# A two-layer hybrid decoder trunk: weight splits and evacuations reordered on the vector engine, expert rows turned one chunk later, a GpSimd multiplication in another form

## What is computed

```python
for l in range(DEPTH):
    h = rmsnorm(x, norm_mix[l])
    qa, ka, va, qb, kb, vb, qi, ki, wi, qc, kc, vc, g = _split(h @ w_in[l], IN_SIZES)
    o_a = stick_breaking_attention(...)       # 4 heads
    o_b = dsa_attention(...)                  # indexer picks the top 64 keys of each query
    o_c = sliding_window_attention(...)       # 8 heads, window 128, learned sinks
    merged = gate0 * (o_a @ w_pa[l]) + gate1 * (o_b @ w_pb[l]) + gate2 * (o_c @ w_pc[l])
    x = x + merged @ w_out[l]
    x = x + cross_attention(...)              # 4 heads into 256 memory tokens
    hf = rmsnorm(x, norm_ffn[l])
    x = x + (swiglu(hf, ...) if l % 2 == 0 else moe_swiglu(hf, ...))   # top 2 of 8 experts
```

## Time and profile before

| | |
|---|---|
| median of 3 runs | 1763.64 us (1762.31 to 1764.25) |
| the profiled execution | 1761.99 us, span 1760.4 us |
| PE busy | 1702.5 us, 97% |
| DVE busy | 1391.7 us, 79% |
| ACT busy | 1104.0 us, 63% |
| POOL busy | 92.9 us, 5% |
| mean transfer rate | 283 GB/s, 366 to 399 GB/s in most slices of the expert loop |

### The profile page before, as it was taken

One profiled execution on the slowest core, in us unless ns is written; L12 is line 12 of the kernel. 1 busy time (PEld: TensorE's weight loads), 2 busy tenths in 40 slices (PEclk: granted clock), 3 DMA queues, 4 the chain that ended last, 5 costly groups with the idle time before them and its releaser, 6 DMA issues.

```text
span 1760.4 us, 22594 instructions
## 1 busy us (share of the span) xinstructions
PE 1702.5 (97%) x7816; PEld 1366.5 (78%) x7816; DVE 1391.7 (79%) x1367; ACT 1104.0 (63%) x1076; POOL 92.9 (5%) x73
## 2 busy tenths in 40 slices
PE   7999898999999999899999999999999999999999
PEld 5777777888777787777888888888888888888876
DVE  5799767545477987668898888888888888888897
ACT  4646355443355453557777777777777777777765
POOL 1100110000001001010000000000000000000440
PEclk9999999999999999999999999999999999999999
DMA  8533494554455335349999999999999999999985
GB/s 301 215 104 130 176 364 149 212 191 169 150 182 182 120 138 204 134 173 399 366 381 366 366 381 369 366 383 365 364 385 363 381 363 368 380 367 366 409 340 195
DMA packets 74113, 498.14 MB, mean 283 GB/s; under 512 B 8256, under 2 KB 9024, under 8 KB 17872
## 3 DMA queue, kind: packets, MB, share of 16 engines
q1 hardware_dynamic: 66560, 467.60, 69.4%
q0 software_dynamic: 7360, 29.87, 4.6%
q10 hardware_dynamic: 144, 0.03, 0.0%
HBM read 481.73 MB, written 15.73 MB: 283 GB/s over the span
## 4 chain that ended last, share of the span: by engine, by line
PE 83%; DVE 8%; ACT 3%; issue 2%; DVEq 2%; DMA 2%; POOL 0%; ACTq 0%; POOLq 0%; SPq 0%
PE ps L588 26%; PE ps L582 26%; PE ps L578 25%; DVE w_lo L416 3%; PE ps L804 1%; ACT w_hi L411 1%; DVE w_lo L1022 1%; PE ps L508 1%; PE ps L1348 1%; DMA rows_of_experts<-scratch,row_no 1%; DVE st L1673 0%; DMA z<-rows_of_experts 0%; DVEq L1676 0%; PE ps L1271 0%; DMA raw<-in_layer_tiles 0%
## 5 line engine op out<-in xcount | busy, mean ns | idle before, releaser
L1022 DVE TENSOR_TENSOR w_lo<-raw,w_hi 128x2048 fp32r<-128x2048 f32 x168 | 391.6, 2332 | 65.9 <-ACT w_hi L939 65.8
L578 PE MATMUL ps<-w_hi,hT_hi 128*128 128x512 f32 (+1 forms) x1520 | 427.1, 403 | 10.4 <-ACT hT_hi L550 4.6
L1022 DVE TENSOR_TENSOR w_lo<-z,w_hi 128x2048 fp32r<-128x2048 f32 x168 | 386.8, 2304 | 45.8 <-ACT w_hi L939 44.7
L588 PE MATMUL ps<-w_lo,hT_hi 128*128 128x512 f32 (+1 forms) x1520 | 413.2, 394 | 7.2 <-DVE w_lo L416 7.1
L582 PE MATMUL ps<-w_hi,hT_lo 128*128 128x512 f32 (+1 forms) x1520 | 413.0, 394 | 1.0 <-DVE hT_lo L557 0.9
L939 ACT ACTIVATE w_hi<-z 128x2048 fp32r<-128x2048 f32 x168 | 321.7, 1915 | 43.2 <-PE ps L588 38.3
L588 PEld LDWEIGHTS ps<-w_lo,hT_hi 128*128 128x128 f32 x1520 | 283.5, 189 | 77.3 <-DVE w_lo L416 9.9
L582 PEld LDWEIGHTS ps<-w_hi,hT_lo 128*128 128x128 f32 x1520 | 284.1, 189 | 70.2 <-DVE hT_lo L557 2.1
L939 ACT ACTIVATE w_hi<-raw 128x2048 fp32r<-128x2048 f32 x168 | 321.0, 1911 | 25.5 <-PE ps L588 25.5
L578 PEld LDWEIGHTS ps<-w_hi,hT_hi 128*128 128x128 f32 x1520 | 272.5, 189 | 67.8 <-ACT hT_hi L550 5.5
L416 DVE TENSOR_TENSOR w_lo<-raw,w_hi 128x2048 fp32r<-128x2048 f32 (+2 forms) x111 | 248.3, 2242 | 77.0 <-ACT w_hi L411 75.2
(11 more groups left out here) (295 smaller groups left out, 993.8 us busy)
## 6 DMA issues: line engine op xcount, KB each, us to landing
z<-in_moe_tiles SPq DMA_DIRECT2D x168, 1024.0 KB, 4.9
raw<-in_moe_tiles SPq DMA_DIRECT2D x168, 1024.0 KB, 4.9
raw<-in_layer_tiles SPq DMA_DIRECT2D x68, 1024.0 KB, 4.9
raw<-in_dense_tiles SPq DMA_DIRECT2D x33, 1024.0 KB, 4.8
rows_of_experts<-z POOLq DMA_DIRECT2D x1, 8704.0 KB, 40.6
raw<-in_layer_tiles SPq DMA_DIRECT2D x8, 512.0 KB, 3.4
z<-rows_of_experts POOLq DMA_DIRECT2D x8, 512.0 KB, 8.1
rows_of_experts<-z POOLq DMA_DIRECT2D x7, 512.0 KB, 6.8
```

The lines of the kernel that those rows point to most:

```text
L578: pe.matmul(acc, hi[:, k, cols], wh, start=start and j == 0, stop=False)
L588: ins = pe.matmul(acc, hi[:, k, cols], wl, start=False, stop=stop and j == len(hk) - 1)
L1022: v.tensor_tensor(w_lo[:, ring, :], moe_raw(p), w_hi[:, ring, :].bitcast(F32), ALU.subtract) \
```

## The change

- GpSimd's four multiplications become tensor_tensor with a broadcast operand.
- `dve_linear` can take a block's first tile before the splits, and does in the first block of layer 1.
- In the first expert, the next expert's rows are transposed, and copied by ACT and DVE, after chunk (1, 1) instead of within it.
- The first gather runs tile by tile, each with its own wait.
- In `pe_program`, one idle product before the last transposes, one before the last logits, one behind them.
- At the start of layer 0, ACT and DVE make the halves of the input before the first weight slot.
- One split goes between the masked scores and the maxima.
- In the merge, the split of slot `last + RING - 1` goes from before the first to before the second evacuation of pb's second block, and the next one to before pc's first.
- In cross-attention, a split goes behind the copy of the first tile's transposed probabilities.
- In the router, both `dve_rows` go later: the first behind the gate difference, the second behind the one-hot table.

```diff
--- before.py
+++ after.py
@@ -345,7 +345,7 @@
                 pool.wait_ge(sem(f"y_back{k}"), 16)
                 if j:
                     pool.wait_ge(sem("x_part"), i + 1)
-                pool.tensor_scalar(yg[:, k, :], yg[:, k, :], g_other[:, j, i:i + 1], None, ALU.mult)
+                pool.tensor_tensor(yg[:, k, :], yg[:, k, :], bc(g_other[:, j, i:i + 1], [P, D]), ALU.mult)
                 pool.drain()
                 pool.tensor_tensor(x_sb[:, i, :], x_sb[:, i, :], yg[:, k, :], ALU.add).then_inc(sem("x_part"), 1)
@@ -618,12 +618,13 @@
                 pe_block_slot(pe, s + n, k0 + 4 * h, h == 0, h == per - 1 or plan[s + n][1] == KC, blk0[name, l] + b, x_lo,
                               hi, lo, between[1] if between and between[0] == n else None)
-        def dve_linear(v, cnt, name, l, take, limit, b0=0, b1=None):
+        def dve_linear(v, cnt, name, l, take, limit, b0=0, b1=None, take_first=False):
             s, nblk, per = slots_of(name, l)
             for b in range(b0, b1 or nblk):
                 last = s + (b + 1) * per - 1
-                ahead(dve_split_to, v, cnt, last - 1, limit)
+                if not take_first:
+                    ahead(dve_split_to, v, cnt, last - 1, limit)
                 blk = blk0[name, l] + b
                 v.wait_ge(sem("tile0_done"), blk + 1)
                 take(b, 0).then_inc(sem("evac"), 1)
@@ -859,8 +860,11 @@
                 pe_moe_chunk(pe, ip, par, 0, 0, ("hg_L", n + 1))
             pe_moe_chunk(pe, ip, par, 0, 1)
             pe_moe_chunk(pe, ip, par, 1, 0)
-            pe_turn_rows(pe, n + 1)
+            if not first_expert(ip, par):
+                pe_turn_rows(pe, n + 1)
             pe_moe_chunk(pe, ip, par, 1, 1)
+            if first_expert(ip, par):
+                pe_turn_rows(pe, n + 1)
             with pe.Fori(2, N_MOE // 2) as u:
                 pe_moe_chunk(pe, ip, par, u, 0)
                 pe_moe_chunk(pe, ip, par, u, 1)
@@ -868,13 +872,13 @@
         def pe_moe(pe):
             pe_idle_products(pe, 2)
             pe.wait_ge(sem("first_hot"), 1)
-            pe.wait_ge(sem("xn_rows"), 2)
-            for k in range(KC):
-                for i in range(TT):
+            for i in range(TT):
+                pe.wait_ge(sem("xn_rows"), i + 1)
+                for k in range(KC):
                     ins = pe.matmul(psG[:, k, :], xn[:, i, k * P:(k + 1) * P], first_hot[:, i, :],
-                                    start=i == 0, stop=i == TT - 1)
-                if k == KC // 2 - 1:
-                    ins.then_inc(sem("first_T"), 1)
+                                    start=i == 0 and k % 4 == 0, stop=i == TT - 1 and k % 4 == 3)
+                    if i and k == KC // 2 - 1:
+                        ins.then_inc(sem("first_T"), 1)
             ins.then_inc(sem("rows_T"), 1)
             pe_expert(pe, 0, 0)
             pe.wait_ge(sem("last_hot"), 1)
@@ -928,7 +932,9 @@
                 chunk(0, 0)
             chunk(0, 1, None if first else "y")
             chunk(1, 0)
-            chunk(1, 1, "rows")
+            chunk(1, 1, None if first else "rows")
+            if first:
+                hook("rows")
             with fori(2, N_MOE // 2) as u:
                 chunk(u, 0)
                 chunk(u, 1)
@@ -1385,10 +1391,10 @@
                     if i == 1 and b == 0:
                         pe_turn_tile(pe, l, 0)
-        def pe_idle_products(pe, n):
+        def pe_idle_products(pe, n, bank=7):
             for _ in range(n):
-                pe.matmul(ps[:, 7, :], ident, x_sb[:, 0, 0:NB], start=True, stop=True)
+                pe.matmul(ps[:, bank, :], ident, x_sb[:, 0, 0:NB], start=True, stop=True)
         def pe_program(pe):
@@ -1445,9 +1451,11 @@
                     pe_turn_half(pe, "mix", x_sb, 0)
                 if l == 0:
                     pe_dense(pe, FFN0[0], N_DENSE, turn_next)
+            pe_idle_products(pe, 1, 0)
             pe_turn_tile(pe, L - 1, 1)
+            pe_idle_products(pe, 1, 0)
             pe_logits(pe, 1)
-            pe_idle_products(pe, 2)
+            pe_idle_products(pe, 1)
             pe.wait_ge(sem("chosen"), 1)
             pe.matmul(ps[:, 6, 0:8], before_tri, chosen[:, 0, :], start=True, stop=True)
             pe.matmul(ps[:, 6, 8:16], ones, chosen[:, 0, :], start=True, stop=False)
@@ -1598,8 +1606,8 @@
                     act.wait_ge(sem("ident_in"), 16)
                     act.activation(warm, ident[:, 0:1], ACT.Copy)
                     act.wait_ge(sem("gains"), 16)
+                    act_hi_gain(act, "mix", l, hT_hi, part=(0,))
                     act_split_to(act, cnt, s0 + 1)
-                    act_hi_gain(act, "mix", l, hT_hi, part=(0,))
                     act.wait_ge(sem("x1_in"), 16)
                     act_squares(act, x_sb, 0, "mix_squares")
                     act_hi_gain(act, "mix", l, hT_hi, part=(1,))
@@ -1766,6 +1774,7 @@
             dve_split_to(v, cnt, g0 + 3)
             dve_gate(v, l, 0, 0)
             dve_masked(v, l, 0, 1, between=0)
+            dve_split_to(v, cnt, g0 + 4)
             dve_row_max(v, l, 1)
             dve_split_to(v, cnt, g0 + 5)
             dve_topk_rounds(v, 0, 1)
@@ -1850,7 +1859,9 @@
                     last = s + (b + 1) * per - 1
                     blk = blk0[name, l] + b
                     for i in range(TT):
-                        if not (j == 1 and b == 0 and i == 1 or j == 2 and b == 1 and i == 1):
+                        if j == 1 and b == 1 and i == 1:
+                            dve_split_to(v, cnt, min(last + RING - 1, lim))
+                        elif not (j == 1 or j == 2 and b == 1 and i == 1) or b == i == 0:
                             dve_split_to(v, cnt, min(last + RING - 1 + i, lim))
                         if i == 0:
                             v.wait_ge(sem("tile0_done"), blk + 1)
@@ -1933,9 +1944,9 @@
             v.drain()
             dve_cross_probs(v, l, 0)
             dve_cross_max(v, l, 1)
-            dve_split_to(v, cnt, s + 3)
             v.wait_ge(sem("x_probs_T"), 2 * l + 1)
             v.tensor_copy(xPT[:, 1, :, 0:P], psXT[0][:, 1, :, :]).then_inc(sem("x_pT_dve"), 1)
+            dve_split_to(v, cnt, s + 3)
             dve_cross_probs(v, l, 1)
             v.wait_ge(sem("x_probs_T"), 2 * l + 2)
             v.tensor_copy(xPT[:, 1, :, P:S], psXT[1][:, 1, :, :]).then_inc(sem("x_pT_dve"), 1)
@@ -1986,15 +1997,13 @@
                     v.tensor_scalar(oh[:, j, i, :], iota[:, 0:8], topi[:, i, j:j + 1], None, ALU.is_equal)
                 if i == 0:
                     dve_rsqrt(v, "ffn", D, norm_rs[:, 6:8])
-                    v.drain()
-                    dve_rows(v, 0)
             v.drain()
             v.tensor_tensor(chosen, oh[:, 0], oh[:, 1], ALU.add).then_inc(sem("chosen"), 1)
             for i in range(TT):
                 v.tensor_tensor(g2[:, i:i + 1], top8[:, i, 1:2], top8[:, i, 0:1], ALU.subtract)
             v.drain()
             v.tensor_tensor(g2[:, 0:2], g2[:, 0:2], norm_rs[:, 6:8], ALU.mult).then_inc(sem("top_two"), 1)
-            dve_rows(v, 1)
+            dve_rows(v, 0)
             v.wait_ge(sem("ranks"), 1)
             ranks = ps[:, 6, 0:16].rearrange("p (t e) -> p t e", t=TT).unsqueeze(1)
@@ -2012,6 +2021,7 @@
             for i in range(TT):
                 ins = v.tensor_scalar(first_hot[:, i, :], iota, slot[:, i:i + 1], None, ALU.is_equal)
             ins.then_inc(sem("first_hot"), 1)
+            dve_rows(v, 1)
             v.tensor_copy(row_no[:, :], row_f.rearrange("p j t -> p (j t)")).then_inc(sem("row_no"), 1)
             v.wait_ge(sem("totals"), 1)
@@ -2063,10 +2073,9 @@
                 s0 = blocks["in", l]
                 if l == 0:
                     v.wait_ge(sem("gains"), 16)
+                dve_lo_gain(v, "mix", l, hT_hi, hT_lo, part=(0,))
                 if l == 0:
                     dve_split_to(v, cnt, s0 + 1)
-                dve_lo_gain(v, "mix", l, hT_hi, hT_lo, part=(0,))
-                if l == 0:
                     v.wait_ge(sem("mix_squares"), 2)
                     dve_rsqrt(v, "mix", D, norm_rs[:, 0:2])
                     dve_lo_gain(v, "mix", l, hT_hi, hT_lo, part=(1,))
@@ -2081,7 +2090,7 @@
                 v.drain()
                 if l == L - 1:
                     v.wait_ge(sem("rows_put"), 16)
-                dve_linear(v, cnt, "in", l, take_in(v), gate0[l], b1=1)
+                dve_linear(v, cnt, "in", l, take_in(v), gate0[l], b1=1, take_first=l > 0)
                 if l == 0:
                     v.wait_ge(sem("mem0_in"), 16)
                     v.wait_ge(sem("mem_squares"), 2)
```

## The result

| | before | after |
|---|---|---|
| median of 11 runs each, taken together | 1765.18 us (1761.79 to 1767.38) | 1769.08 us (1767.35 to 1771.37) |
| ratio, with its 95% interval | | 1.0026 (1.0018 to 1.0034) |
| the profiled execution (span) | 1761.99 (1760.4) | 1768.96 (1767.4) |

The changed kernel is slower by 0.26%, some 4.6 us (3.2 to 6.0). The two profiled executions lie 7.0 us apart.

What follows compares the result with a forecast made beforehand. TensorE was taken as the bound, busy 97% of the span, with VectorE about 12% from being the bound in the expert loop. Terms summed to +3.8 us, giving 1767.4 us, range 1761.0 to 1771.0.

Steps and rivals of the forecast that it cites:

- GpSimd's form: Last stage: tensor_tensor multiplications hold DVE longer and PE waits for aT_lo; +3.5 us (0 to +5).
- Start: Layer 0, first products: input halves made before the first split let PE start 0.85 earlier; -0.75 us (0 to -1.3).
- Low half between scores and maxima, cross-attention copy: Mixers and cross-attention: PE's wait only changes cause, or ACT's copy still sets PE's start; 0 us each.
- Merge and take first: Merges, both layers: evacuations before splits, -1.85 us; layer 1's first block: wait moves by one tile, -0.05 us.
- Router: Router and gather: idle products fill idle time, PE's second gather group starts 0.7 earlier; -0.7 us, +1.5 if clock stays low.
- rival D: Clock also falls in the router or the stretched GpSimd stage; +2 to +3 us on top, 1770; chance 0.09 with E.
- GpSimd's scatters start as now: Router and gather: the scatters' start was taken as unchanged by the edits.
- Turning: First expert: rows turned a chunk later save a 1.38 wait, but late copies leave no splits ahead; +3.65 us (-1.4 to +4).
- A: Broadcast multiplication holds DVE no longer than tensor_scalar; +0.3 us, 1763.9, not slower; chance 0.18.
- B: ACT's queue has more cover at the first expert's handover than seen; -1.25 us in all, 1762.4; chance 0.09.
- C: Both A and B hold; -4.8 us, 1758.9, faster; chance 0.06.
- E: No gains, each freed wait reappears; main case without -3.3 us, 1770.7; chance 0.09 with rival D.

Runs made afterwards that it cites:

- e6: The kernel before with only GpSimd's four multiplications changed to tensor_tensor; 1767.23 us, ratio 1.0019 to the kernel before.
- e7: The kernel before with only the first expert's turning and copies of the next rows one chunk later; 1767.04 us, ratio 1.0017 to the kernel before.
- e5: e3 with two idle products behind the second logits instead of one; 1762.52 us, ratio 0.9993 to the kernel before.
- e3: The changed kernel with both GpSimd's multiplications and the turning of the rows as before; 1760.85 us, ratio 0.9982 to the kernel before.
- e8: e3 with the router's idle products as before: none ahead of last transposes and logits, two behind; 1763.39 us, ratio 0.9997 to the kernel before.
- e2: The changed kernel with the next expert's rows turned and copied within chunk (1,1) again; 1764.66 us, ratio 1.0003 to the kernel before.
- e1: The changed kernel with GpSimd's four multiplications as tensor_scalar again; 1765.82 us, ratio 1.0010 to the kernel before.
- e9: e3 with rows turned between chunk (1,1)'s gate/up slots, copies at its end, two idle products behind the second logits; 1759.41 us, ratio 0.9973.

## Why the prediction was right, and where it was not

The sum of +3.8 stands against +4.6 (3.2 to 6.0) by the ratio. Read by stages, two profiles are not enough: the kernels of e6 and e7 run the same program as before until the first expert, and reached the first mark at 762.42 and 762.62, not 759.58. At the products behind the second slots they were already 1.8 to 1.9 us behind: their first three groups took 2.07, 2.08 and 1.91, where the profile of before shows 2.07, 1.81 and 1.10. Of this, 0.5 to 0.6 was there before PE's first product (13.34 and 13.26 against 12.73), and the rest is the clock, which rose earlier in the profile of before. So the profile on which I made the sum was a fast execution. With means over all executions that share a stage's program (the first three rows of the table: three before, seven changed for the first mark, five for the router) the steps are:

| step | forecast | measured |
|---|---|---|
| to the router (start, take first, merge) | -2.65 | -3.0 (761.54 to 758.57) |
| router and gather | -0.7 | +0.7 (24.15 to 24.86) |
| first expert, turning, with the wait for the rows | +3.65 | +3.2 |
| GpSimd's form | +3.5 | +3.7 |
| sum | +3.8 | +4.6 |

That the sum is off by only 0.8 is in part luck. The start gave 1.0 us more than forecast and the first expert cost 0.5 less; the merges gave 0.7 less, the router lost 1.4 against its forecast, and the form cost 0.2 more. The first mark also varies between executions, from 759.6 to 762.6 before and from 757.8 to 759.4 after.

- **Start**: forecast -0.75, measured -1.8 (mean of the products behind the second slots, 23.68 to 21.90). Counted from the first transposes, PE's first product came 5.55 us later in six of the seven changed executions, against 6.3 to 6.8 before: the 0.75, as worked out. In the changed kernel's own profile it came after 6.06, at 12.87, later than before and not near the forecast 11.9, since ACT's first split began only at 10.81, when the slot had landed. My sum left out a second gain. In the kernel before, PE waited again behind its first group:

```profile
15.25 1.81 PE L582 MATMUL ps<-w_hi,hT_lo 128*128 128x512 f32 x4 [0.44 <-DVE hT_lo L557]
```

  Now that DVE makes hT_lo before it splits, this wait is gone, and the second group starts 1.84 behind the first instead of 2.52: -0.7. What is left, some -0.6, is the clock's rise, and +0.3 is that the input landed later in these executions (7.01 against 6.67 on average).
- **Low half between scores and maxima, cross-attention copy**: both forecast 0. The gate evacuation took the place of w_lo (3.39 became 3.41), and ACT's copy still released PE. Right in mechanism and size.
- **Merge and take first**: forecast -1.9; between the second slots and the first mark the means differ by 1.2 (737.86 to 736.67), and part of that is the clock: e6 has two groups at the lower level in layer 0's merge (1.85 and 1.91, from 207.60 on; granted clock 0.91 from 203 to 222), where after has 1.00. The two profiles alone differ by 0.35. The wait in layer 1's first block moved by one tile (1.49 became 1.46 at 498.94), as forecast. By the two profiles the merge of layer 0 won 0.6 (PE's tile at 213.48, where 213.70 less the 0.39 of the start was expected) and that of layer 1 0.8, against 0.8 and 1.05. I followed DVE's chain alone and had not named the wait for the low half at 205.12 (1.16), which comes of the split standing one evacuation later.
- **Router**: the step that failed. It took "with idle products the clock is up" as given, with +1.5 as the bound if not. The logits were warm (1.92), but one idle product behind them left a hole of 1.54 us, and the clock fell there instead: the two idle products ahead of the gather held PE to 770.1, 2.4 us after DVE's table was ready (767.7). e5 shows that one product more keeps the clock at 1.00 and brings 1.8 us. In part this is rival D.
- **The scatters.** The step "GpSimd's scatters start as now" was wrong. The scatters start 1.3 us earlier (0.6 of it inside the router's stage), the third takes 1.5 less, PE comes later out of the router, and so the wait of 1.38 for the rows was gone whether or not the rows were turned later (e3, e8). The later turning would have removed it too (e7). My step booked -1.38 to the turning: the sum is the same, the cause is not. Both cancel in the total: without the turning my account gives +0.15, and e2 measured +0.5; without the form as well it gives -3.3, and e3 measured -3.2.
- **Turning**: ACT copies at s+1.07 (forecast 1.13), PE goes on at s+3.95 (4.0), with s = 806.74. The down product's second group, which I put at s+11.4 at the full clock and 0.7 later at the lower one, starts at 818.63, s+11.9, and without a wait. e7, where the clock stays up, shows the forecast waits at about half their size: 0.19 for w_lo (0.43) and 0.40 for aT_lo (0.76), the latter at s+11.3. The clock's part, 0.7 forecast, is 0.6 by e1 and e7. Gross 4.7 against my 5.05.
- **GpSimd's form**: the size, 3.5 against 3.7, is nearly right, the picture only in part. I had a multiplication hold DVE for 2.35 and GpSimd get its turn at PSUM instructions alone. In the trace the two engines alternate one by one, also between two adjacent splits (8.05 for two, 2.28 each alone), and each GpSimd operation from the first addition on lengthens a split by 1.4 to 1.8. The last addition ends at 1694.3; my chain, moved by the 3.3 us of the stages ahead, would end it at 1703.8. The waits that I put at 1698.6 and 1708.0 are not there. Earlier ones are longer instead (2.73, 0.47 and 2.57 against 2.14, 0.86 and 0.79 before: +2.0), and 3.41 us of lower clock behind the last bring the rest. Two errors of the step cancelled. By the last stage the term is 3.3 us (e2 less e3, 113.0 and 109.75), 3.8 (e6 less before) or 5.2 (after less e1); by the runs it is 3.8, 3.4 and 2.8 for the same pairs. So 3.5 us is inside what can be told, and no closer.

What the Trainium skill says in "SBUF — State Buffer", section "Who interferes with whom", fits the alternation of these operations: the splits have two SBUF inputs, and each of the two engines waits for the other's whole instruction. It has no difference between GpSimd's two forms, and the traces show one: beside tensor_scalar the splits took 2.8 to 2.9, beside tensor_tensor 3.6 to 4.1. In sizing, the measurement decides. What the Trainium skill says in "GPSIMD Engine Reference", section "Engine selection", which rates two-input operations the slower ones, does not fit the operation's own duration. The first of the four took 1.91 as tensor_tensor and 2.88 as tensor_scalar. Neither ran alone: the tensor_tensor made the split beside it 2.88 long, and the tensor_scalar left its split at 2.29. Shorter by itself and dearer for its neighbour: both stand in these two traces. Why tensor_scalar costs DVE so little I did not settle.

The rivals: A, B and C are out by e1 and e7. D came true in the router and, for 3.41 us, in GpSimd's stage. E holds for the mixers and the cross-attention copy only.

## What to carry to other kernels

An edit that cures a wait should be tried alone and with its neighbours: here two edits removed the same wait for the rows, and one of them cost 4.7 us for it; only the kernel without that one showed it. A stage that becomes faster meets its neighbours at another time, and they can pay: e5 won 1.8 us in the router and lost 5.75 in its profile behind it. When an operation must wait for another engine, look at what is queued behind it, and place the producer ahead by the length of that cover, as e9 does with the transposes, a gate/up slot and a down slot ahead of the copies. Judge an operation on a shared path by what its neighbour's instructions last beside it, not by its own duration.

## What was not expected of the hardware

- Three executions of one program differ by 1.9 us at the products behind the second slots (22.43 to 24.34). Most of it is when TensorE's clock rises: the third group of four took 1.10 in one and 1.91 in two others. 0.5 to 0.6 was there before. One profile is not a mean to make a sum of 4 us against.
- The same hole of 2.91 us was followed by 3.41 us of the lower clock in one kernel (groups of 1.70 and 1.91) and by none in another.
- GpSimd's multiplication with a broadcast operand took 1.91 as the first of four and 3.94 among DVE's splits; tensor_scalar took 2.88 as the first, then 4.89, 4.88 and 7.00. Of the two the shorter one made the later splits 0.8 to 1.2 us longer than the other did.
- The issue of an indirect DMA by GpSimd waits for DVE's split, so far as the timing shows it. The third scatter took 0.96 in five profiles, where no split was under way when it began, and 2.47 or 2.48 in the eight others. Where one was, the issue ended 0.84 to 0.86 us behind the split's end: at 775.62 behind 774.77 in e5, at 777.44 behind 776.60 in the kernel before, at 772.80 behind 771.94 and 777.14 behind 776.30 in e3. It was not tried by itself.
